# The gate columns of the odd layer: weights stand and tokens stream, and four modulation rows move to the output linear

## The reference

```
qkv, g, a_in, b_in = split_cols(a @ w_in, (2048, 1024, 16, 16))
log_a = -exp(a_log) * softplus(a_in + dt_bias)
beta  = sigmoid(b_in)
```

## Time and profile before

| | |
|---|---|
| Median of 3 runs | 2228.63 us (2227.8 to 2230.28) |
| The profiled execution's own time | 2229.53 us |
| Its span | 2227.8 us |
| TensorE, VectorE, ScalarE, GpSimd busy | 92%, 68%, 40%, 6% |
| Mean granted TensorE clock | 0.943 |

### The profile page before, as it was taken

How to read it: one execution, slowest core, us unless ns; L and a number is a source line. 1 busy time by engine, 2 the same in 40 slices (tenths; PEclk the granted TensorE clock), 3 DMA queues, 4 the chain that set the end, 5 groups by cost and what they waited for, 6 DMA issues and landing times. The chain is left out here.

```text
span 2227.8 us, 40146 instructions
## 1 busy us (share of the span) xinstructions
PE 2048.6 (92%) x16858; PEld 1831.8 (82%) x16858; DVE 1507.7 (68%) x2320; ACT 901.8 (40%) x1338; POOL 140.4 (6%) x231
## 2 busy tenths in 40 slices
PE   6998987999999799899988999798899989988997
PEld 5786865788888588688886999698799979887997
DVE  6866566998676758656646777768666666956454
ACT  3436443222222433322325444546444355554443
POOL 0100000011000011201210000000000000000000
PEclk7999989999999889899998999899899999988999
DMA  8532022455553366100003777343357734323552
GB/s 329 200 125 76 1 95 95 176 184 190 187 187 115 117 227 221 45 3 3 3 21 114 256 276 277 106 145 102 125 207 276 275 111 155 130 95 111 181 183 92
DMA packets 59133, 323.94 MB, mean 145 GB/s; under 512 B 6384, under 2 KB 7536, under 8 KB 32624
## 3 DMA queue, kind: packets, MB, share of 16 engines
q1 hardware_dynamic: 33360, 228.97, 29.2%
q0 software_dynamic: 25344, 92.29, 11.8%
q10 hardware_dynamic: 288, 0.66, 0.1%
HBM read 320.84 MB, written 1.05 MB: 144 GB/s over the span
## 5 line engine op out<-in xcount | busy, mean ns | idle before, releaser
L370 DVE TENSOR_TENSOR w_low<-raw,w_high 128x1024 fp32r<-128x1024 f32 (+1 forms) x408 | 473.4, 1202 | 243.5 <-ACT w_high L362 243.2
L362 ACT ACTIVATE w_high<-raw 128x1024 fp32r<-128x1024 f32 (+1 forms) x408 | 402.5, 1035 | 397.6 <-PE banks L407 389.2
L548 DVE SCALAR_TENSOR_TENSOR mod_rows<-mod_rows,silu_condition 128x1024 f32<-128x1024 f32 x176 | 212.9, 1221 | 14.3 <-DMA mod_rows<-rows_dram 11.7
L405 PE MATMUL banks<-ffn_a_l,w_high 128*128 128x256 f32 x704 | 199.7, 284 | 1.9 <-DVE ffn_hidden L1006 1.9
L406 PE MATMUL banks<-ffn_a_h,w_high 128*128 128x256 f32 x704 | 199.1, 283 | 0.0
L407 PE MATMUL banks<-ffn_a_h,w_low 128*128 128x256 f32 x704 | 199.1, 283 | 0.0
L405 PE MATMUL banks<-mlp_a_l,w_high 128*128 128x512 f32 (+1 forms) x512 | 176.7, 345 | 11.9 <-DVE mlp_a_l L690 7.7
L534 POOL DMA_DIRECT2D mod_rows<-rows_dram x176 | 93.2, 530 | 1368.4 <-DVE mod_rows L548 1152.1
L406 PE MATMUL banks<-mlp_a_h,w_high 128*128 128x512 f32 (+1 forms) x512 | 175.2, 342 | 0.0
L407 PE MATMUL banks<-mlp_a_h,w_low 128*128 128x512 f32 (+1 forms) x512 | 174.9, 342 | 0.0
L405 PE MATMUL banks<-mlp_hidden_l,w_high 128*128 128x512 f32 (+1 forms) x512 | 173.3, 338 | 1.3 <-DVE mlp_hidden_l L1014 1.3
(11 more groups left out here) (598 smaller groups left out, 4876.4 us busy)
## 6 DMA issues: line engine op xcount, KB each, us to landing
raw<-panels_dram SPq DMA_DIRECT2D x204, 1024.0 KB, 4.8
mod_rows<-rows_dram POOLq DMA_DIRECT2D x176, 512.0 KB, 5.1
mod_0a_rows<-rows_dram SPq DMA_DIRECT2D x8, 1024.0 KB, 19.4
x_features<-x_features_dram SPq DMA_DIRECT2D x1, 2048.0 KB, 11.3
constants<-small_dram SPq DMA_DIRECT2D x1, 1672.5 KB, 6.8
silu_condition<-conditions_dram SPq DMA_DIRECT2D x2, 512.0 KB, 12.5
out_dram<-x_features SPq DMA_DIRECT2D x4, 256.0 KB, 2.1
constants<-small_dram SPq DMA_DIRECT2D x1, 736.5 KB, 5.4
```

The costliest lines, as they stand in the source:

```text
L362: self.nc.scalar.activation(self.wh[:, m % 2, cols], self.raw[:, slot, cols], ACT.Copy).then_inc(self.w_high, 1)
L370: self.nc.vector.tensor_tensor(self.wl[:, m % 2, cols], self.raw[:, slot, cols], self.wh[:, m % 2, cols].bitcast(F32), ALU.subtract).then_ ...
L405: self.nc.tensor.matmul(out, sh(k), ml(k), start=(opens and k == 0), stop=False)
L548: nc.vector.scalar_tensor_tensor(row if v == nv - 1 else self.scratch[:], row, 1.0, self.cond[v][:], ALU.mult, ALU.mult, accum_out=mod[:, ...
```

## The change

The gates' product is turned round. `narrow` lets the 32 columns of the weight stand and streams all 512 tokens: one block of 24 products instead of four blocks of 24. The result, 32 x 512 with gates on the partitions, goes by ScalarE into a free part of the convolution buffer `pre`. At panel 1 of `odd_v` TensorE turns it with four transposes of 32 x 128 into PSUM bank 7 (`turn_narrow`, `turn_ab`), and the gate steps read it there, where `odd_ab` stood in SBUF. `gate_inputs` now waits for that turn.

The rows: `odd_g` has 1, 1, 2 and 2 instead of 2, 2, 2 and 2; the gates' linear has none instead of 2; the four panels of `odd_out` have one each instead of none. 6 + 12 + 12 = 30 stand ahead of the rule, 4 in `odd_out`, and 30 in the MLP as before. VectorE empties no block of the gates' linear any more, ScalarE the only one.

`info` now keeps the free marks of the banks that a linear did not use, so that `odd_v` still sees who emptied banks 1 to 3.

```diff
@@ linear
-            info.update(done=done, taken=taken, bank_free=bank_free)
+            kept = prior["bank_free"] if prior is not None else {}
+            info.update(done=done, taken=taken, bank_free={**kept, **bank_free})
@@ new in Program
+    def narrow(self, high, low, n, width, nk):
+
+        def product(q, m, bank):
+            return self.product3(bank[0:width, 0:n],
+                                 lambda k: self.wh[:, m % 2, k * width:(k + 1) * width],
+                                 lambda k: self.wl[:, m % 2, k * width:(k + 1) * width],
+                                 lambda k: high[:, k, 0:n], lambda k: low[:, k, 0:n], nk)
+        return product
+
+    def turn_narrow(self, pe, src, out, width):
+
+        for i in range(src.shape[1] // P):
+            last = self.nc.tensor.transpose(out[:, i * width:(i + 1) * width], src[:, i * P:(i + 1) * P],
+                                            self.c("ident")[0:width, 0:width])
+        return last
@@ odd_mixer
-    ab = pr.sb("odd_ab", [P, 4, 32], ctx=inner)
+    ab = ps[:, 7, 0:P].rearrange("p (i n) -> p i n", n=32)
...
-                        beside=lambda which, eng, p: beside(which, eng, 2))
-    ab_ready = pr.linear("odd_ab_in", 1, 4, 4, pr.tokens(high, low, 4, 32, KD),
-                         pr.copy_out(lambda q: ab[:, q, :]), [], prior=g_info, info=ab_info,
-                         beside=lambda which, eng, p: beside(which, eng, 2))
+                        beside=lambda which, eng, p: beside(which, eng, 1 + p // 2))
+    ab_ready = pr.linear("odd_ab_in", 1, 1, 1, pr.narrow(high, low, N, 32, KD),
+                         lambda q, which, eng, bank: nc.scalar.activation(pre[0:32, 7, :], bank[0:32, :], ACT.Copy), [],
+                         engines=("act",), prior=g_info, info=ab_info)
+    ab_turned = pr.sem("odd_ab_turned")
+
+    def turn_ab(pe):
+        for w in ab_ready:
+            pe.wait_ge(*w)
+        pr.turn_narrow(pe, pre[0:32, 7, :], ps[:, 7, 0:P], 32).then_inc(ab_turned, 1)
@@ gate_inputs
-        for w in ab_ready:
-            dve.wait_ge(*w)
+        dve.wait_ge(ab_turned, 1)
@@
-    gate_steps = {("dve", 1): gate_inputs, ("act", 1): gate_logs, ("dve", 2): log_decays}
+    gate_steps = {("dve", 1): gate_inputs, ("act", 1): gate_logs, ("dve", 2): log_decays,
+                  ("pe", 1): turn_ab}
@@ layer1
-            take, _ = pr.row_work("mod2_0a", [(2 * N_MOD, 34, 1, pr.mod2[0], 0, b_mod[0])], slots, [], silu_ready)
+            take, _ = pr.row_work("mod2_0a", [(2 * N_MOD, 30, 1, pr.mod2[0], 0, b_mod[0])], slots, [], silu_ready)
...
+            take_rest, rest = pr.row_work(
+                "mod2_0b", [(2 * N_MOD + 30, 18, 1, pr.mod2[0], 30, b_mod[0]),
+                            (3 * N_MOD, 16, 1, pr.mod2[1], 0, b_mod[1])], slots, [pr.after_rule], [])
             ready = pr.linear("odd_out", 4, 2, 8, pr.features(high, low, TL, KD, tall_offset),
-                              pr.add_gated(mod, 16, 1, TL), y_split, engines=("dve",), rising=True)
+                              pr.add_gated(mod, 16, 1, TL), y_split, engines=("dve",), rising=True,
+                              beside=lambda which, eng, p: take_rest(eng, 1) if which == "dve" else None)
...
-            ready = mlp(1, mod, 1, TL, ready, lambda t: pr.row_work(
-                "mod2_0b", [(2 * N_MOD + 34, 14, 1, pr.mod2[0], 34, b_mod[0]),
-                            (3 * N_MOD, 16, 1, pr.mod2[1], 0, b_mod[1])], slots, [pr.after_rule], []), {1: 1, 2: 1})
+            ready = mlp(1, mod, 1, TL, ready, lambda t: (take_rest, rest), {1: 1, 2: 1})
```

## The result

The changed kernel takes **2214.77 us** (median of 7 runs, 2212.45 to 2220.22) against 2230.28 us for the kernel before on the same chip (7 runs, 2227.8 to 2233.76): a ratio of 0.9935, 95% interval 0.992 to 0.995. The forecast was 2215.6, range 2212.5 to 2221.5. The profiled execution took 2212.54 us, with a span of 2210.8.

A forecast was written before the change was run, and what follows sets the result against it. TensorE, busy 92% of the span, was taken as the bound. `odd_v` effectively starting at 798.15 instead of 811.64 gives 13.5, less 0.5 for the turn: 13.0 us, so 2215.6 us, range 2212.5 to 2221.5.

The forecast's parts named there:

- The new product: Gates' linear: 24 products of 512 streamed columns, 0.234 each, 5.6 us, ending at 796.95.
- The clock: Gates' product into `odd_v`: stays at 1.00 over a TensorE standstill of about 1.2 us.
- Rival B: Gates' product: the clock falls all the same; gain 11.0 (2217.6 us), or 6.1 (2222.5) at half clock throughout; chance 0.13.
- on the safe side: Before `odd_v`: a 1.2 us wait keeps the clock, as 1.50 us left it at 1.00 and 2.46 us 0.54.
- Start of `odd_v`: First product of `odd_v` at 798.15, set by VectorE's split, 0.45 after ScalarE; bounds 797.7 and 800.3.
- I take these 8.2 us: Last row of `odd_g`: its load takes 8.2 us from issue, as in the trace, so it is there at 794.4.
- The turn: Panel 1 of `odd_v`: four 32 x 128 transposes cost 0.5 us on the path (0.2 to 1.0).
- Rows in `odd_out`: Four rows in `odd_out` cost zero: each fits VectorE's idle time of 1.79 us, leaving 0.6 us of cover.
- rival C: Behind the changed stretch: slack there gives part of the gain back; gain 0 to 4 us, 2226.5 us; chance 0.06.
- Rival A: Last row of `odd_g` lands at 796.5, `odd_v` starts at 800.3, clock falls; gain 9.1, 2219.5 us; chance 0.20.
- The base: Whole kernel: profiled execution of 2229.53 us, 0.9 above the median of 2228.63, from which the gain is taken.

The follow-up runs named there:

- the rows with 256 columns: Against the kernel before: four rows moved to `odd_out`, the gates' old 96 products kept but streaming 256 columns instead of 32; 2221.86 us, ratio 0.9971.
- the pair above: Two kernels with the old 96 gates' products and rows moved to `odd_out`, streaming 32 columns (2226.96 us) or 256 (2221.86 us).
- rows alone: Against the kernel before: four rows moved to `odd_out`, the gates' old product with 32 streamed columns kept; 2226.96 us, ratio 0.9996.
- form alone: Against the kernel before: the new gates' product and its turn, modulation rows left where they were; 2223.05 us, ratio 0.9974.
- wide `mix_small`: The changed kernel with `mix_small_in` streaming 256 columns instead of 32 in both layers of the second block; 2212.3 us, ratio 0.9921 to the kernel before.

## Why the prediction was right

Its mechanism held but for one step, the wait that releases `odd_v`, and the sum is right (13.0, measured 13.1): `odd_v` began 0.3 sooner than forecast and the turn was 0.14 shorter, and some 0.3 of that is not found again at the rule. To compare places, 4.04 us are added to the times after, so that `odd_g` begins with before's.

- **The new product**: forecast 5.6 us, ended 796.95. Measured 0.23 from start to start, ended 797.08. With 32 columns standing, a stream of 512 takes as long as with 128.
- **The clock**: forecast to hold. It did, and the rows with 256 columns show that the reason given, the thin stream, was the cause. Rival B falls. That a wait of 1.2 us is "on the safe side" was not put to the test, as the wait was 0.77, and the traces do not bear it out as a rule: a wait of 1.56 us elsewhere was followed by a fall (last section).
- **Start of `odd_v`**: forecast 798.15, decided by VectorE's split. Measured 797.85, decided by ScalarE's emptying (forecast 797.7 for that). The failing step is the term "I take these 8.2 us": the load took 6.2. The last row was there at 792.8, not at 794.4 as forecast, though its load was issued at 786.7, 0.5 later than forecast. In the eight profiled executions with this spread of rows it took 5.8 to 6.6 in five, 7.5 in one, 8.3 and 8.4 in two. Only above 7.3 does it reach the path, as VectorE had 1.1 us to spare at 6.2: at 7.45 TensorE's idle time was 0.90, at 8.40 it was 1.83, and 0.77 at 6.2 or less. The forecast took the one duration it had seen, and this was at the long end.
- **The turn**: forecast 0.5, measured 805.58 - 805.22 = 0.36.
- **Rows in `odd_out`**: forecast zero, with a cover of 0.6. Measured 0.1, which is within what this stretch varies by; the cover is 0.64, and what happens beyond the cover was measured (2.6).
- **Nothing given back** (rival C): 1309.8 and 1310.0 us behind the stretch. That the two agree to 0.2 is luck, as the part repeats to some 2.6 us.
- **Rival A** did not decide the median, but it exists: one execution had it. Its price was forecast as 3.9 us over the forecast and measured as 2.4, as the row landed at 8.4 us and not at 10.4.
- **The base.** The forecast started from a profiled execution 0.9 over the median of three runs. The kernel before had medians of 2226.9 to 2230.5 on the chips used here, and `odd_g` begins up to 9 us apart in executions of kernels that are alike up to there. L of the changed kernel is known to some 0.1 when no row is late, that of the kernel before from one execution, in which the row that decides took 8.2 us; in two others with the same rows it took 8.7. The absolute time is not known to better than some 2 us, and the medians fell by 15.5 us on one chip and 10.5 on the other. That the forecast of 2215.6 lies 0.8 from the median of 2214.77 is therefore in part luck: it started 1.65 below the median that the kernel before has over seven runs.

What the forecast did not say is how little each half is worth: 6.6 for the form, 1.0 for the rows, 13.1 for both. The form shortens TensorE's work and runs into the rows; the rows clear VectorE but leave the thin stream. And some half of the gain is the clock's, 6.5 by the pair above: the old products with 256 columns and the rows moved give 8.8 of the 13.1, the wait of 2.75 included, with more streamed columns than before.

## What to carry to other kernels

Where a product streams few columns, look at the granted clock inside it before counting products: here streaming eight times the columns with the same instructions won 6.5 us (7.8 less the wait of 1.3), while 24 products in place of 96 are worth 96 x 0.11 - 24 x 0.23 = 5.0 at full clock. Look for all its places; a second one gave another 6 us of the profiled execution with one changed width. When a wait and a slow stretch stand together, remove both or expect half or less, and ask what the engine behind the wait is itself waiting for, with the longest duration seen, not one.

## What the runs showed of the hardware

- The clock fell in unbroken streams of 128x32 products (796.5, 1458.7; 795.4 with rows alone; 18 of 18 in `mix_small`) but not in the streams of 128x256 put in their place, nor in those of 512 columns against 32 standing ones.
- Waits: in the stretches compared above the clock fell during or behind 1.83, 3.01 and 5.54 us, and not behind 0.77 or 1.56 (1.00 to 1458 there). The length alone does not decide. The same instruction waits 1.56 us in the kernel before (at 227.96) and in the changed one (at 226.01); the clock stayed at 1.00 to 232 in the first and fell in the second. And in the form alone it stayed up over 3.34 us. First the changed kernel, then the form alone, each with the window behind the wait (columns as rows 2):

```profile
226.01 0.68 PE L1555 MATMUL banks<-constants,even_pa 128*128 128x128 f32 x4 [1.56 <-ACT even_pa L1627]
226.50:229.90 3.40, 3.40 (x32) 1.90 (x30) 0.86 (x2) 1.79 (x5) 0.00 (x0) 0.50 0.02 5
...
1438.52 0.48 PE L2660 MATMUL banks<-mix_rot,constants 128*128 128x256 f32 x1 [3.34 <-ACT mix_rot L2656]
1438.50:1453.00 14.50, 14.48 (x120) 14.23 (x120) 13.34 (x24) 8.73 (x15) 0.00 (x0) 1.00 0.62 214
```

- A product of 32 streamed columns takes 0.11 us from start to start, one of 256 takes 0.12, both at a clock of 1.00; at 0.50 the one of 32 takes 0.21.
- The second of two 512 KB row loads, beside 1 MB panels, took 5.8 to 8.7 us from one execution to the next. In the 6.16 us of the changed kernel 2.47 MB moved (400 GB/s), in the 8.33 us of the rows alone 2.54 MB (305 GB/s), with the two queues' packets taking 100% and 85% of the engines' time. In the 8.4 us of the wide `mix_small` 3.09 MB moved (368 GB/s), so a load can be late with more traffic as well as with a lower rate. Why like traffic runs at two rates is open.
